# A gated recurrent layer in a three-block network: values of the context projected between the norms, ahead of the queries, and the gating unit's mixing inside the branch projection

## The reference

```
h_ctx = modulate(rmsnorm(ctx));  h = modulate(rmsnorm(x))
q, ff, fb, v, g, u, sv, ga, gb = split(h @ w_in)     # ff, fb and v for h_ctx too
q = silu(q)
f = lb + (1 - lb) * sigmoid(ff or fb);  k = 1 - f;  b = cumsum(log f)     # both directions
state = sum over the context of (k * exp(b_last - b))^T v
o = decayed scores(q, k) @ v + (q * exp(b)) @ state          # both directions added
y_a = (rmsnorm(o) * silu(g)) @ w_branch_a
mixed = w_s @ rmsnorm(gelu(sv)) + b_s;  y_b = (gelu(u) * mixed) @ w_branch_b
x = x + g_m * ((sigmoid(ga) * y_a + sigmoid(gb) * y_b) @ w_out)
x = x + g_f * experts(modulate(rmsnorm(x)))          # 16 experts, 32 tokens each
```

## Time and profile before

| | |
|---|---|
| time, median of 3 runs | 2498.96 us (2498.46 to 2502.54) |
| profiled execution: time, span | 2497.85 us, 2496.1 us |
| PE, PE weight load | busy 82%, 51% of the span |
| DVE, ACT, POOL | busy 30%, 18%, 1% |
| granted PE clock, mean | 0.913 of full speed |
| DMA | 614.98 MB, mean 246 GB/s |

### The profile page before, as it was taken

The page is one execution under the profiler, slowest core; times in us unless marked ns, Lnnn a source line. Parts: engine busy times, 40 slices in busy tenths (PEclk is TensorE's granted clock), DMA queues, the critical chain, the costliest instruction groups (busy, mean ns, idle before and its releaser), DMA issues.

```text
span 2496.1 us, 28771 instructions
## 1 busy us (share of the span) xinstructions
PE 2038.2 (82%) x11807; PEld 1281.0 (51%) x11807; DVE 760.5 (30%) x1671; ACT 445.4 (18%) x963; POOL 12.6 (1%) x23
## 2 busy tenths in 40 slices
PE   6998899999999999999999999665655555556565
PEld 3544368888747857899877777222211111111111
DVE  3217745555401556685037522200000000000001
ACT  3004534010101446311033221000000000000000
POOL 0000000000000000000000000000000000000000
PEclk9999999999999999999999989878888788777778
DMA  9557861331321531354522326799999999999997
GB/s 382 203 202 283 323 237 34 102 101 47 86 79 42 151 118 35 130 153 117 203 99 93 135 77 236 302 427 428 427 428 427 428 428 428 428 427 428 427 428 324
DMA packets 181171, 614.98 MB, mean 246 GB/s; under 512 B 26192, under 2 KB 121680, under 8 KB 147248
## 3 DMA queue, kind: packets, MB, share of 16 engines
q1 hardware_dynamic: 180224, 610.38, 62.4%
q0 software_dynamic: 816, 2.76, 0.4%
HBM read 612.06 MB, written 1.05 MB: 246 GB/s over the span
## 4 chain that ended last, share of the span: by engine, by line
PE 59%; DMA 34%; DVE 4%; ACT 2%; issue 1%; SPq 0%; POOL 0%; DVEq 0%; ACTq 0%
PE ps L388 57%; DMA ring<-in_expert_w_up 13%; DMA ring<-in_expert_w_gate 11%; DMA ring<-in_expert_w_down 8%; DMA ring<-in_ab_w_in 1%; PE ps L809 1%; DVE ST L844 1%; DVE X L756 0%; DVE AR L755 0%; ACT AR L862 0%; ACT AR L874 0%; DVE H L707 0%; DVE AR L896 0%; DVE ps L843 0%; PE ps L538 0%
## 5 line engine op out<-in xcount | busy, mean ns | idle before, releaser
L388 PE MATMUL ps<-ring,AR 128*32 128x256 f32 (+2 forms) x4336 | 567.7, 622 | 354.7 <-DMA ring<-in_expert_w_up 129.7
L388 PEld LDWEIGHTS ps<-ring,AR 128*32 128x32 f32 (+1 forms) x4336 | 192.8, 134 | 705.4 <-issue 238.2
L388 PE MATMUL ps<-H,ring 128*128 128x256 f32 (+2 forms) x2240 | 512.4, 387 | 7.9 <-ACT H L693 5.1
L388 PEld LDWEIGHTS ps<-H,ring 128*128 128x128 f32 x2240 | 403.0, 191 | 103.7 <-issue 55.0
L388 PE MATMUL ps<-AR,ring 128*128 128x256 f32 (+2 forms) x1548 | 359.7, 390 | 3.9 <-DVE AR L999 2.9
L388 PEld LDWEIGHTS ps<-AR,ring 128*128 128x128 f32 x1548 | 273.5, 191 | 84.4 <-issue 53.1
L2294 DVE TENSOR_TENSOR AR<-AR,ps 128x512 f32<-128x512 f32 x16 | 11.0, 688 | 583.0 <-PE ps L388 583.0
L388 PE MATMUL ps<-AR 128*128 128x128 f32 (+7 forms) x1200 | 172.6, 336 | 19.1 <-ACT AR L862 8.6
L388 PEld LDWEIGHTS ps<-AR 128*128 128x128 f32 (+4 forms) x1200 | 127.2, 181 | 50.7 <-issue 44.5
L2280 ACT ACTIVATE AR<-ps 128x512 f32<-128x512 f32 x16 | 9.6, 597 | 522.7 <-PE ps L388 522.7
L2311 DVE TENSOR_TENSOR AR<-ps,X 32x256 f32<-32x256 f32 x60 | 25.2, 420 | 253.7 <-PE ps L388 252.1
(11 more groups left out here) (297 smaller groups left out, 1447.1 us busy)
## 6 DMA issues: line engine op xcount, KB each, us to landing
ring<-in_expert_w_gate SPq DMA_DIRECT2D x64, 2048.0 KB, 23.3
ring<-in_expert_w_down SPq DMA_DIRECT2D x63, 2048.0 KB, 23.2
ring<-in_expert_w_up SPq DMA_DIRECT2D x61, 2048.0 KB, 23.3
ring<-in_ada_w SPq DMA_DIRECT2D x36, 2048.0 KB, 10.4
ring<-in_ffn_w SPq DMA_DIRECT2D x44, 1024.0 KB, 7.6
ring<-in_w_in SPq DMA_DIRECT2D x12, 2048.0 KB, 7.8
ring<-in_ffn_w SPq DMA_DIRECT2D x16, 1408.0 KB, 7.0
ring<-in_ab_w_in SPq DMA_DIRECT2D x4, 2048.0 KB, 16.0
```

Of the source, the lines that this page charges most:

```text
L388: m = nc.tensor.matmul(out_, lhsT=lhsT, rhs=rhs, start=start, stop=stop)
```

## The change

Four things are moved. No arithmetic is added or taken away.

1. The job of the value weights (columns 1536 to 2048 of `w_in_2`) goes ahead of that of the query weights in the list of loads.
2. The values of the context's two pieces are projected beside the norms, with `pre2a[0]`'s sum between them (it moves from behind the last context chunk of `fz` to behind the first of these pieces); ACT copies them within `act_norms`.
3. The values of `x`'s two pieces follow the eight `fz` chunks, and the queries come last.
4. The mixing goes from ahead of branch a's projection to between its chunks 3 and 4, on PE and on DVE.

```diff
-            c = [512, 1024, 0, 1536, 2048, 2560, 3072, 3584, 4096, 4608, 5120][i]
+            c = [512, 1024, 1536, 0, 2048, 2560, 3072, 3584, 4096, 4608, 5120][i]
...
         def pe_hgrn_in(pe):
+            def values(t):
+                w = weights(pe, ("in2", 2)).rearrange("p (k n) -> p k n", k=KD)
+                b = take(pe, ("v2", t))
+                for k in range(KD):
+                    mm(ps[:, b, :], H[:, k, t * P:(t + 1) * P], w[:, k, :], k == 0, k == KD - 1, b if k == KD - 1 else None)
...
-                        if part == 1 and h % 3 == 0:
-                            (pre2a[0] if h else post1f).pe(pe)
+                        if part == 1 and h == 0:
+                            post1f.pe(pe)
                     if part == 0:
                         used()
-            w = weights(pe, ("in2", 2)).rearrange("p (k n) -> p k n", k=KD)
+                    else:
+                        values(2)
+                        pre2a[0].pe(pe)
+                        values(3)
+            for t in range(2):
+                values(t)
+            used()
+            w = weights(pe, ("in2", 3)).rearrange("p (k n) -> p k n", k=KD)
             for h in range(HH):
                 pe_dense(pe, ("q2", h), w, h * P, H, TX)
             used()
...
+                if n in (9, 15):
+                    values(2 + n // 15)
...
+            for t in range(2):
+                values(t)
             for h in range(HH):
                 b = full_of(c.eng, ("q2", h))
...
-            for t in range(4):
-                b = full_of(c.eng, ("v2", t))
-                c.free(S.activation(V2[:, t, :], ps[:, b, :], ACT.Copy), ("v2", t))
-                if t % 2 == 0:
-                    act_left(c, t // 2)
+            for d in range(2):
+                act_left(c, d)
...
             for n in range(KD):
                 pe_dense(pe, ("ya", n), w, n * P, O2, TX, K=4)
+                if n == 3:
+                    for t in range(2):
+                        pe.wait_ge(sv_ready, t + 1)
+                        b = take(pe, ("mix", t))
```

More of the change, by code:

```diff
@@ L1617, in pe_hgrn_in, with values @@
             used()
-            w = weights(pe, ("in2", 3)).rearrange("p (k n) -> p k n", k=KD)
-            for t in range(4):
[L1620 to L1623, removed]
         def act_hgrn_in(c):
+            def values(t):
+                b = full_of(c.eng, ("v2", t))
+                c.free(S.activation(V2[:, t, :], ps[:, b, :], ACT.Copy), ("v2", t))
             def raw(n):
@@ L1886, in pe_gates @@
             freed(pe, "wst")
[L1887 to L1893, removed]
             pe.wait_ge(o_ready.sem, og_o + 4)
@@ L1897, in pe_gates @@
                 pe_dense(pe, ("ya", n), w, n * P, O2, TX, K=4)
+                if n == 3:
+                    for t in range(2):
+                        pe.wait_ge(sv_ready, t + 1)
+                        b = take(pe, ("mix", t))
+                        for g in range(4):
+                            mm(ps[:, b, g * P:(g + 1) * P], ft("ones", P, 1), SGB[0:1, g * P:(g + 1) * P], True, False)
+                            mm(ps[:, b, g * P:(g + 1) * P], sv(t, g), WST[:, g, :], False, True,
+                               b if g == 3 else None)
             used()
@@ L1969, in dve_gates @@
             c.eng.wait_ge(gates_ready, 5)
[L1970 to L1973, removed]
             for n in range(KD):
@@ L1976, in dve_gates @@
                 c.free(V.tensor_tensor(YA[:, n, :], gate(n), ps[:, b, 0:TX], ALU.mult), ("ya", n))
+                if n == 3:
+                    for t in range(2):
+                        b = full_of(c.eng, ("mix", t))
+                        u = U2[:, :, t * P:(t + 1) * P]
+                        c.free(V.tensor_tensor(u, u, ps[:, b, :].rearrange("p (g t) -> p g t", g=4), ALU.mult), ("mix", t))
             for n in range(KD):
```

## The result

| | before | changed |
|---|---|---|
| time, median | 2502.11 us (6 runs, 2498.46 to 2502.54) | 2510.67 us (6 runs, 2509.1 to 2513.51) |
| ratio to before | 1 | 1.0042 (95%: 1.0032 to 1.0052) |
| span of the profiled execution | 2496.1 us | 2508.0 us |
| PE, DVE, ACT busy | 82%, 30%, 18% | 81%, 30%, 18% |
| granted PE clock, mean | 0.913 | 0.911 |

The changed kernel is slower by 0.42%, some 10.5 us (8 to 13). This ratio is as recorded; the two medians lie 8.6 us apart (0.34%), still within its interval. More runs of the kernel before put its median at 2502.11 instead of the 2498.96 that stood ahead of the forecast, so 2504.2 was forecast for a change of +5.3 us on a base that was 3 us low.

A forecast was written before the change was run, and what follows sets the result against it. PE's work ahead of a fixed DMA stream of expert weights was taken to set the end. Late transposes +13.1 (6.2 gained included), clock +2.7, gating unit -10.5 gave +5.3 us: 2504.2 us, range 2500.3 to 2510.

The forecast's parts named there:

- part 2: Gating unit, mixing moved inside branch a: branch b starts 10.5 us sooner, with the clock expected to hold.
- The norms' gaps: Start of the recurrent layer: values beside the norms leave PE nothing to wait for, gaining 6.2 us.
- The wait behind the queries: Ahead of the first transposes: PE waits 19.3 us for the ACT and DVE chain, so they come 13.1 us later.
- The clock behind the wait: Restart at the transposes: half clock costs 2.7 us, with 1.8 and 3.7 as its ends.
- The idle time ahead of the mixing: Gating unit: PE's idle 3.04 us shrink to 0.4, with the operand ready under cover of branch a's first chunks.
- The mixing: Gating unit: at full clock it takes 5.7 us instead of 11.4, bounds 3.5 and 11.4.
- the second rival: Mixing: the exposed weight load does not scale with the clock; +7.4 us in all, 2506.4 us, chance 0.11.
- Branch a's second half: Behind the mixing at the gating unit: 6.9 us instead of 9.2.
- The first rival: Gating unit: the clock falls within the mixing and slows branch a behind it; +10 us in all, 2509, chance 0.17.
- The base: Whole kernel before: profiled execution 2497.85 us, the three runs' median 1.1 above it, to which the change was added.

The follow-up runs named there:

- one_piece: Changed kernel with only one context piece of values beside the norms, the other three pieces between queries and transposes: 2488.16 us, ratio 0.995.
- q_ahead: Changed kernel with the queries projected ahead of the values of x instead of behind them: 2497.79 us, ratio 0.9985.
- after_wide: Changed kernel with the bias of a tile added by one matmul of 512 columns: 2506.0 us, ratio 1.0016.
- mix_wide: one_piece with the bias of a tile added by one matmul of 512 columns instead of four of 128: 2483.21 us, ratio 0.9927.
- p2_only: Kernel before with only the mixing moved between chunks 3 and 4 of branch a: 2494.51 us, ratio 0.9972.
- before_wide: Kernel before with only the bias of a tile added by one matmul of 512 columns, mixing at its old place: 2496.67 us, ratio 0.9982.
- mix_nobias: one_piece with the bias left out of the mixing, so the output lacks it: 2479.14 us, ratio 0.9912.

## Why the prediction was wrong

The direction and the wait were right, and the size was not: the measured time is just above the range, and the change of 10.5 us (8.6 by the medians) is up to twice the forecast's. The step that failed is the one on part 2: "I expect the clock to hold: it was 1.00 from 296 to 302 us with PE busy only 2.71 of 6 us". Its term of -10.5 us came out as -4.8, and as -6.4 at best in the other traces with the same rows. The clock fell within the mixing, and a pair at full clock was dearer than forecast.

- **The norms' gaps.** Right: no gap from the first chunk on. The 6.2 us are in the table's +13.0, and one_piece shows them without the wait.
- **The wait behind the queries.** Right to 0.2 us: 19.11 against 19.3. q_ahead shows its cause.
- **The clock behind the wait.** Forecast 2.7. In the changed trace the transposes and the chunk behind them take 1355.74 - 1349.07 = 6.67 us, against 1338.18 - 1333.85 = 4.33 in the kernel before (the next transposes start at 1338.18 there), a loss of 2.3. Another 1.1 us came back at the later gap of 4.14 us, where the clock rose sooner (8.74 us for the 32 records instead of 9.84). Why it rose sooner there was not tested.
- **The idle time ahead of the mixing.** Right: 0.40 us, and branch a's first half 7.1 against 6.9.
- **The mixing.** Forecast 5.7 us, measured 8.96. Two errors. A pair at full clock takes 0.416 us, not 0.36: the exposed part fell from 0.27 to about 0.20, so it neither halves nor stays whole as in the second rival. Over 16 pairs that is 1.0 us. (The loads themselves did not halve either: 0.50 us for the two of a pair at half clock, 0.29 to 0.30 at full clock in the changed kernel's trace.) And from the ninth pair on the clock is at half: those eight take 1502.71 - 1497.08 = 5.63 us instead of 3.33, 2.3 more. The prediction itself gave 11.4 us as an upper bound of the mixing, but its own range used only the lower one, 3.5.
- **Branch a's second half.** Forecast 6.9, measured 9.21: the clock returns only about 4.6 us into it. That is 2.3 us more.
- **The first rival.** It was this one, priced at +10 for the whole, with a chance of 0.17. That +10 comes so close to 10.5 is in part luck: the price lacked the 1.0 us of the pairs, and it did not have the 1.1 us that came back at the later gap. What spoke against this rival was one row in which PE had gaps between other matmuls. That row said nothing of the pattern at hand. It also ended too early. From 296 to 302 us the clock was 1.00 in all eleven traces, but in eight of them it fell within the next 4 us, so its average from 300 to 306 us was below 1.00.
- **The base.** Three runs gave 2498.96, and the profile of before reached the layer earliest of all eleven traces. Nothing in one trace says so. The low base put the forecast's time 3 us low and, together with a range whose upper end was set just above this rival's price on the low base, left the result outside by 0.7 us.

after_wide tests the account. There the mixing is over almost before the clock falls, the stretch is 10.2 us shorter than before, and the total is +4.0 us (4.5 by the medians), in the forecast's own range. That 10.2 is so near the forecast's 10.5 is luck in part: the wide mixing is 0.8 us shorter than the 5.7 forecast, and the remaining loss to the clock is 1.7. But it shows that nothing outside this stretch was missed by more than a microsecond or two.

What makes the clock fall is shown only so far. A block of the mixing brought it in five traces (3.2 to 4.3 us after its start) and the same pairs spread out did not. The block of 128-row matmuls at 1342.5 us, without one-row matmuls, did not bring it in 5.4 us. This points at the one-row matmuls, but no run has a longer block without them in that place. What in the block the clock's control reacts to was not separated.

## What to carry to other kernels

Before a projection is moved to fill a gap, look at what it covered where it was: the two gaps, 3.9 us together, could be filled with one piece of values out of four, and the other three were worth 19 us as cover for the chain behind the queries. Between tiny matmuls, count the changes between row counts, not the columns: adding the bias of a tile by one wide matmul instead of four narrow ones was worth 4.5 us in the kernel before and 5 to 6 in one_piece. mix_wide, with both lessons in it, is 18.3 us faster than the kernel before (ratio 0.9927), which puts it some 28 us below the changed one.

## What was not expected of the hardware

- A PE that is listed as busy without a gap can lose its clock. It fell 3.3 us (changed kernel) and 4.3 us (p2_only) into a block of alternating one-row and 128-row matmuls that began at full clock, and in the mixing at half clock it never rose in 11.4 us. The same rows can come out differently: with the wide bias it fell 3.2 us in (after_wide) or not at all in 4.2 us (mix_wide).
- A change between a one-row and a 128-row matmul costs 0.20 us at 2.4 GHz and 0.27 to 0.30 at 1.2 GHz (the first from mix_wide and the changed kernel, the second from before_wide and before). In a run of matmuls over the same 128 rows the loads show nowhere (0.11 us a record in mix_nobias).
- With the same instructions ahead of it, the same matmul started up to 4.6 us apart in different traces; in the late ones the clock had fallen between 300 and 306 us, in the early ones it had not.
